# Second attention: high and low parts of the later heads spread over units, the other half's key rows copied on chip

## What is computed

```python
def diff_attend(q, k, v, lam):
    s = jnp.einsum('bqhmd,bkhmd->bhmqk', q, k, preferred_element_type=jnp.float32)
    a = jax.nn.softmax(s * (1.0 / math.sqrt(ATTN_HEAD_DIM)), axis=-1)
    a = a[:, :, 0] - lam * a[:, :, 1]
    return jnp.einsum('bhqk,bkhe->bqhe', a.astype(v.dtype), v)
```

## Time and profile before

| | us |
|---|---|
| median of 3 runs (2997.75 to 3001.31) | 2998.06 |
| profiled execution | 2997.38 |
| its span | 2996.1 |
| busy in the span: PE / DVE / ACT / POOL | 2786.9 / 1625.8 / 1218.2 / 289.7 |
| mean granted clock of PE | 0.973 |

### The profile page before, as it was taken

One profiled execution on the slowest core, in us unless ns is written; L12 is line 12 of the kernel. 1 busy time (PEld: TensorE's weight loads), 2 busy tenths in 40 slices (PEclk: granted clock), 3 DMA queues, 4 the chain that ended last, 5 costly groups with the idle time before them and its releaser, 6 DMA issues.

```text
span 2996.1 us, 36001 instructions
## 1 busy us (share of the span) xinstructions
PE 2786.9 (93%) x14288; PEld 2331.1 (78%) x14288; DVE 1625.8 (54%) x1933; ACT 1218.2 (41%) x1794; POOL 289.7 (10%) x397
## 2 busy tenths in 40 slices
PE   6999999999999999999999999978889399999994
PEld 5788888788888888888888888867778288888883
DVE  3277776432343323233334532367764688888985
ACT  3244443511232212122123412157762177777773
POOL 1011110000000000000002000023331300010002
PEclk9999999999999999999999999989999599999997
DMA  5100001111313222222232411000012589999994
GB/s 170 32 22 22 10 23 43 36 49 50 106 51 91 76 65 85 70 79 78 71 102 73 150 38 50 22 1 1 36 58 85 203 305 397 397 397 391 397 395 171
DMA packets 228103, 366.83 MB, mean 122 GB/s; under 512 B 11117, under 2 KB 158337, under 8 KB 227937
## 3 DMA queue, kind: packets, MB, share of 16 engines
q1 hardware_dynamic: 214688, 322.08, 30.4%
q0 software_dynamic: 13248, 42.45, 4.6%
HBM read 339.21 MB, written 25.28 MB: 122 GB/s over the span
## 4 chain that ended last, share of the span: by engine, by line
PE 73%; issue 16%; DVE 6%; ACT 2%; POOL 2%; DMA 1%; SPq 0%; ACTq 0%; DVEq 0%; POOLq 0%
PE ps L469 71%; DVE misc L2295 2%; POOL misc L947 1%; PE ps L548 1%; PE ps L2732 0%; PE ps L2753 0%; DVE r L2678 0%; ACT r L444 0%; DVE f L2619 0%; DVE f L2950 0%; DVE f L2617 0%; DVE f L2620 0%; DMA f<-in_x_dram 0%; ACT f L2218 0%; POOL f L2356 0%
## 5 line engine op out<-in xcount | busy, mean ns | idle before, releaser
L469 PE MATMUL ps<-r,r 128*128 128x512 f32 (+2 forms) x10824 | 2378.8, 377 | 27.3 <-DVE r L453 6.1
L469 PEld LDWEIGHTS ps<-r,r 128*128 128x128 f32 x10824 | 1928.4, 189 | 386.6 <-DVE r L453 12.5
L444 ACT ACTIVATE r<-f 128x1024 fp32r<-128x1024 f32 (+2 forms) x410 | 573.6, 1417 | 486.6 <-PE ps L469 484.3
L453 DVE TENSOR_TENSOR r<-f,r 128x1024 fp32r<-128x1024 f32 (+3 forms) x222 | 249.9, 1143 | 534.3 <-ACT r L444 534.1
L2678 DVE TENSOR_TENSOR r<-f,r 128x2048 fp32r<-128x2048 f32 x188 | 429.0, 2290 | 66.6 <-ACT r L444 65.3
L469 PE MATMUL ps<-f,f 128*128 128x128 f32 (+5 forms) x1538 | 245.6, 306 | 4.9 <-ACT f L2548 3.7
L469 PEld LDWEIGHTS ps<-f,f 128*128 128x128 f32 (+1 forms) x1538 | 204.2, 200 | 22.4 <-issue 15.7
L731 DVE SCALAR_TENSOR_TENSOR f<-f,misc,f 128x1023 f32<-128x1023 f32 (+29 forms) x120 | 146.3, 1261 | 0.0
L1583 ACT ACTIVATE r<-f 128x512 fp32r<-128x512 f32 x44 | 27.8, 632 | 210.1 <-DVE f L1605 210.1
L2218 ACT ACTIVATE f<-ps,misc 128x1280 f32<-128x1280 f32 x64 | 85.2, 1331 | 63.4 <-DVE misc L2295 63.4
L1015 ACT ACTIVATE f<-ps,misc 128x128 f32<-128x128 f32 (+7 forms) x64 | 47.5, 742 | 151.8 <-DVE misc L1004 151.8
(11 more groups left out here) (269 smaller groups left out, 1797.1 us busy)
## 6 DMA issues: line engine op xcount, KB each, us to landing
f<-in_w_gate_dram SPq DMA_DIRECT2D x64, 1024.0 KB, 8.3
f<-in_w_up_dram SPq DMA_DIRECT2D x64, 1024.0 KB, 10.4
f<-in_w_down_dram SPq DMA_DIRECT2D x64, 1024.0 KB, 8.2
f<-in_w_in_dram SPq DMA_DIRECT2D x56, 512.0 KB, 3.9
f<-in_w_ada_dram SPq DMA_DIRECT2D x48, 512.0 KB, 3.5
f<-in_w_ffn_in_dram SPq DMA_DIRECT2D x44, 512.0 KB, 4.7
f<-in_w_ffn_out_dram SPq DMA_DIRECT2D x18, 512.0 KB, 3.8
f<-in_w_out_dram SPq DMA_DIRECT2D x16, 512.0 KB, 3.5
```

The lines of the kernel that those rows point to most:

```text
L444: self.act.activation(st.hi[st.slot[i]][:, 0:n], st.raw[i % len(st.raw)][:, 0:n], ACT.Copy).then_inc(self.sem(st.name + "_hi"), 1)
L453: self.dve.tensor_tensor(st.lo[s][:, 0:n], st.raw[i % len(st.raw)][:, 0:n], st.hi[s][:, 0:n].bitcast(F32), ALU.subtract).then_inc(self.sem ...
L469: return self.pe.matmul(o, left, right, start=start, stop=stop, skip_group_check=True)
```

## The change

The high parts of the other rows are no longer made by ACT, and POOL's subtractions are gone. DMAs copy the own rows of K, L and C to the other rows: for head 0 on POOL's queue, for heads 1 to 3 on SP's, ahead of the loads of the output weights, which now wait for the high and low parts alone. PE waits for 96 counts (six DMAs) of `dma_k0` to `dma_k3` at a head's first scores. `act_stack` and `dve_stack` take a list of parts; the tables `HIGH_AT` and `LOW_AT` tell at which unit, counted from the start of the head before, each is made. For head 1 the high parts stand in units 2 to 5 and the low ones in 4 to 6; for heads 2 and 3 the high parts in units 1 to 5 and the low ones in 2 to 6 of the head before. For head 0 only the dealing of the work changes. Semaphores that share a number are regrouped.

```diff
@@ -1951,53 +1951,78 @@
 
 
 
-    def act_stack(self, h, mp):
-
-        act, sem = self.act, self.sem
+
+
+    HIGHS = [["Q0", "K0", "C0", "Q1", "K1", "C1"], ["K1", "C1", "Q0", "Q1", "K0", "C0"]] + 2 * [
+        ["Q0", "Q1", "K0", "C0", "C1", "K1"]]
+    LOWS = [["Q0", "K0", "C0", "Q1", "K1", "C1"], ["Q0", "Q1", "K1", "K0", "C0", "C1"]] + 2 * [
+        ["Q0", "Q1", "K0", "C0", "C1", "K1"]]
+
+    HIGH_AT = {2: "K1 C1", 3: "Q0", 4: "Q1", 5: "K0 C0"}, {1: "Q0", 2: "Q1", 3: "K0", 4: "C0 C1", 5: "K1"}
+    LOW_AT = {4: "Q0", 5: "Q1 K1", 6: "K0 C0 C1"}, {2: "Q0", 3: "Q1", 4: "K0", 5: "C0 C1", 6: "K1"}
+
+    def high_count(self, h, part):
+        return 6 * h + self.HIGHS[h].index(part) + 1
+
+    def low_count(self, h, part):
+        return 6 * h + self.LOWS[h].index(part) + 1
+
+    def stacked(self, h, part):
+
+        x, mp = part[0], int(part[1])
         own, other = ((slice(0, 64), slice(64, 128)), (slice(64, 128), slice(0, 64)))[mp]
         sk = self.stacks[h % 2]
-        act.activation(sk["Q"][mp][own, :], self.Q2[own, h, :], ACT.Copy).then_inc(sem("sk_hi"), 1)
-        for k, c in ((self.K2[own, h, :], slice(0, 1024)), (self.K2c[own, h, :], slice(1024, 1280))):
-            act.activation(sk["K"][mp][own, c], k, ACT.Copy).then_inc(sem("sk_hi"), 1)
-            act.activation(sk["K"][mp][other, c], k, ACT.Copy).then_inc(sem("sk_hi"), 1)
-
-    def low_keys(self, h, mp):
-
-        own = (slice(0, 64), slice(64, 128))[mp]
-        sk = self.stacks[h % 2]
-        return ((self.K2[own, h, :], sk["K"][mp][own, 0:1024], sk["L"][mp]),
-                (self.K2c[own, h, :], sk["K"][mp][own, 1024:1280], sk["C"][mp]))
-
-    def dve_low_queries(self, h, mp):
-
-        own, other = ((slice(0, 64), slice(64, 128)), (slice(64, 128), slice(0, 64)))[mp]
-        sk, n = self.stacks[h % 2], 5 * (2 * h + mp)
-        self.dve.wait_ge(*self.sem("sk_hi", n + 1))
-        self.dve.tensor_tensor(sk["Q"][mp][other, :], self.Q2[own, h, :], sk["Q"][mp][own, :].bitcast(F32),
-                               ALU.subtract).then_inc(self.sem("sk_lo"), 1)
-
-    def dve_low_keys(self, h, mp):
-
-        own = (slice(0, 64), slice(64, 128))[mp]
-        if h % 2 and mp:
-            self.dve.wait_ge(*self.sem("sk_lo", 3 * (2 * h + mp) + 1))
-        for j, (k, high, low) in enumerate(self.low_keys(h, mp)):
-            self.dve.wait_ge(*self.sem("sk_hi", 5 * (2 * h + mp) + 2 + 2 * j))
-            self.dve.tensor_tensor(low[own, :], k, high.bitcast(F32), ALU.subtract).then_inc(self.sem("sk_lo"), 1)
-
-    def pool_low_keys(self, h, mp):
-
-        other = (slice(64, 128), slice(0, 64))[mp]
-        if h % 2 and mp:
-            self.pool.wait_ge(*self.sem("sk_lo", 3 * (2 * h + mp) + 1))
-        for j, (k, high, low) in enumerate(self.low_keys(h, mp)):
-            self.pool.wait_ge(*self.sem("sk_hi", 5 * (2 * h + mp) + 2 + 2 * j))
-            self.pool.tensor_tensor(low[other, :], k, high.bitcast(F32), ALU.subtract).then_inc(self.sem("sk_lp"), 1)
-            self.pool.wait_ge(*self.sem("sk_lp", 2 * (2 * h + mp) + j + 1))
-
-    def dve_stack(self, h, mp):
-        self.dve_low_queries(h, mp)
-        self.dve_low_keys(h, mp)
+        if x == "Q":
+            return self.Q2[own, h, :], sk["Q"][mp][own, :], sk["Q"][mp][other, :], other
+        if x == "K":
+            return self.K2[own, h, :], sk["K"][mp][own, 0:1024], sk["L"][mp][own, :], other
+        return self.K2c[own, h, :], sk["K"][mp][own, 1024:1280], sk["C"][mp][own, :], other
+
+    def act_stack(self, h, parts):
+
+        for part in parts:
+            src, high, _, _ = self.stacked(h, part)
+            self.act.activation(high, src, ACT.Copy).then_inc(self.sem("sk_hi"), 1)
+
+    def dve_stack(self, h, parts):
+
+
+        for part in parts:
+            src, high, low, _ = self.stacked(h, part)
+            self.dve.wait_ge(*self.sem("sk_hi", self.high_count(h, part)))
+            if h == 1 and part == "K1":
+                self.dve.wait_ge(*self.sem("sk_lo", self.low_count(h, "Q1")))
+            self.dve.tensor_tensor(low, src, high.bitcast(F32), ALU.subtract).then_inc(self.sem("sk_lo"), 1)
+
+    def copy_high_keys(self, queue, h, mp):
+
+        other = self.stacked(h, f"K{mp}")[3]
+        own = slice(64 - other.start, 128 - other.start)
+        k = self.stacks[h % 2]["K"][mp]
+        queue.wait_ge(*self.sem("sk_hi", max(self.high_count(h, f"K{mp}"), self.high_count(h, f"C{mp}"))))
+        queue.dma_start(k[other, :].bitcast(F32), k[own, :].bitcast(F32)).then_inc(self.sem(f"dma_k{h}"), 16)
+
+    def copy_low_keys(self, queue, h, part):
+        other = self.stacked(h, part)[3]
+        own = slice(64 - other.start, 128 - other.start)
+        k = self.stacks[h % 2]["L" if part[0] == "K" else "C"][int(part[1])]
+        queue.wait_ge(*self.sem("sk_lo", self.low_count(h, part)))
+        queue.dma_start(k[other, :].bitcast(F32), k[own, :].bitcast(F32)).then_inc(self.sem(f"dma_k{h}"), 16)
+
+    def sp_stacks(self):
+
+        sp = self.sp
+        self.copy_high_keys(sp, 1, 1)
+        self.copy_low_keys(sp, 1, "K1")
+        self.copy_high_keys(sp, 1, 0)
+        for part in ("K0", "C0", "C1"):
+            self.copy_low_keys(sp, 1, part)
+        for h in (2, 3):
+            self.copy_high_keys(sp, h, 0)
+            for part in ("K0", "C0", "C1"):
+                self.copy_low_keys(sp, h, part)
+            self.copy_high_keys(sp, h, 1)
+            self.copy_low_keys(sp, h, "K1")
 
 
 
@@ -2022,8 +2047,7 @@
         act, sem = self.act, self.sem
         act.wait_ge(*sem("rp", 16))
         act.wait_ge(*sem("kc", 4))
-        self.act_stack(0, 0)
-        self.act_stack(0, 1)
+        self.act_stack(0, self.HIGHS[0])
         for ct in range(4):
             for n in range(3):
                 self.high(self.ws, self.i_cv + 3 * ct + n + 3)
@@ -2035,17 +2059,15 @@
 
     def dve_conv2(self):
         dve, sem, ps, u = self.dve, self.sem, self.ps, self.u2
-        self.dve_stack(0, 0)
-        self.dve_low_queries(0, 1)
+        self.dve_stack(0, ("Q0", "K0", "C0", "Q1"))
         for ct in range(4):
             o = self.CV[ct]
             self.low(self.ws, self.i_cv + 3 * ct + 4)
             if ct == 3:
 
                 dve.wait_ge(*sem("w_lo", len(self.ws.items)))
-                self.dve_low_keys(0, 1)
+                self.dve_stack(0, ("K1", "C1"))
                 dve.wait_ge(*sem("sk_lo", 6))
-                dve.wait_ge(*sem("sk_lp", 4))
             for hf in range(2):
                 dve.wait_ge(*sem("cv2_mm", 6 * ct + 2 + hf + 1))
                 dve.wait_ge(*sem("c2_u", 2 * ct + hf + 1))
@@ -2077,12 +2099,16 @@
             pool.dma_start(self.lams[:, i * 64:(i + 1) * 64], a[name].to_broadcast([P, 64])).then_inc(sem("lam"), 16)
 
     def pool_conv2(self):
-        self.pool_low_keys(0, 0)
+        pool = self.pool
+        self.copy_high_keys(pool, 0, 0)
+        self.copy_low_keys(pool, 0, "K0")
+        self.copy_low_keys(pool, 0, "C0")
+        self.copy_high_keys(pool, 0, 1)
         self.pool.wait_ge(*self.sem("mod_row", 4))
         self.pool.dma_start(self.rows_dram.rearrange("r (c p) -> (r c) p", p=P),
                             self.row_parts[0][64:96, :]).then_inc(self.sem("dma_kept"), 16)
-        self.pool.wait_ge(*self.sem("w_lo", len(self.ws.items)))
-        self.pool_low_keys(0, 1)
+        self.copy_low_keys(pool, 0, "K1")
+        self.copy_low_keys(pool, 0, "C1")
 
     def dve_lambda(self):
         dve, sem, lam, c, t = self.dve, self.sem, self.lams, self.lamc, self.lt
@@ -2137,9 +2163,9 @@
             if u:
                 pe.wait_ge(*sem(f"a2_exp{mp}", u))
             if i == 0:
-                pe.wait_ge(*sem("sk_hi", 5 * (2 * h + 2)))
-                pe.wait_ge(*sem("sk_lo", 3 * (2 * h + 2)))
-                pe.wait_ge(*sem("sk_lp", 2 * (2 * h + 2)))
+                pe.wait_ge(*sem("sk_hi", 6 * (h + 1)))
+                pe.wait_ge(*sem("sk_lo", 6 * (h + 1)))
+                pe.wait_ge(*sem(f"dma_k{h}", 96))
             q = sk["Q"][mp][:, i * P:(i + 1) * P]
             for c in range(3):
                 cs = slice(c * 512, min(c * 512 + 512, 1280))
@@ -2274,13 +2300,14 @@
                     act.wait_ge(*sem("cv2_mm", 24))
                 ct = (u + 3) % 4
                 act.activation(self.MX[0][:, 4 + ct, :], self.CV[ct], ACT.Copy).then_inc(sem("mc_hi"), 1)
-            for h, at in ((1, 4), (2, NT + 1), (3, 2 * NT + 1)):
-                if u == at:
-                    act.wait_ge(*sem("mc_lo", 4))
-                    act.wait_ge(*sem("a2_qk1", u + 1 if h == 1 else NT * (h - 1)))
-                    self.act_stack(h, 0)
-                if u == at + 1:
-                    self.act_stack(h, 1)
+            for h in range(1, 4):
+                parts = self.HIGH_AT[h > 1].get(u - NT * (h - 1), "").split()
+                if parts and h > 1:
+
+                    act.wait_ge(*sem("a2_qk1", NT * (h - 1)))
+                elif parts and u > 2:
```

(25 more changed lines are left out.)

## The result

The changed kernel takes 2972.51 us (median of 4 runs, 2970.34 to 2973.99) against 2999.68 (4 runs) for the kernel before: 27.2 us less, ratio 0.9900, 95% interval 0.9887 to 0.9912. Forecast were 33.7 less, 2964.4, with a range of 2958 to 2979. The sign and the mechanism were right, and so was the place but for unit 3, which the change made longer; 6.5 us of the gain are missing.

What follows compares the result with a forecast made beforehand. PE's matmuls were taken as 71% of the chain of waits, leaving only PE's waits in the stack stretches to win; gains of 11.3, 11.3 and 11.1 us off 2998.06 gave 2964.4 us, range 2958 to 2979.

Steps and rivals of the forecast that it cites:

- Where the loss sits: Second attention, units 4 to 24: stretches holding stacks of heads 1 to 3 exceed plain 6.34 us units by 43.1 us.
- High parts, 3.1 us a head: Heads 2 and 3: ACT's remaining high parts lie in both unit loops; 3.1 us a head stay, bounds 2.5 to 5.0.
- Low parts, nothing: DVE's low parts, a unit after their high parts, cost nothing, covered by its 1.28 us wait for PE's first scores.
- rival B: Stack units: each high part with its low part still costs 2.2 us, fifteen cost 33, gain 10: 2988 us; 6%.
- Copies hidden: On-chip copies before each head's first scores: last lands in 3.2 us against 4.8 of room, so nothing is waited for.
- Rivals C and D: Head starts: C, last copy lands late, 2985 us, 9%; D, a copy runs on one DMA engine, 3040 us, 3%.
- Heads 2 and 3: Units 9 to 16 and 17 to 24: 64.95 us becomes about 53.8; gains 11.3 and 11.1 us.
- Head 1: Units 4 to 8: 34.6 us for 46.24, less 0.3 lost earlier; gain 11.3, between 9.5 and 12.5.
- K1 C1 in unit 2 ... +0.2 to 0.3: Units 2 and 3: head 1's high parts delay ACT's next copies, partly covered by 1.32 us idle; +0.2 to 0.3 us.
- Rival A: Fifteen stack units: short PE idles drop its clock to 1.2 GHz, 0.9 us a unit, 14 us: 2978 us; 12%.
- Sum: Whole kernel: gains of 11.3, 11.3 and 11.1 us for heads 1, 2 and 3 make 33.7, arriving whole: 2964.4 us.

Runs made afterwards that it cites:

- copies alone: Changed kernel with on-chip copies kept, but high and low parts bunched again into two units a head, lows with their highs: 2988.84 us, ratio 0.9958.
- spreading alone: Changed kernel with parts still spread over units, but heads 1 to 3 without copies: ACT makes high keys twice, POOL subtracts again; 2994.75 us, ratio 0.9977.

## Why the prediction was right, and where it was off

**Where the loss sits** held. The gain lies in the stretches of heads 1 to 3, and the 43.1 us there were the ceiling; outside them only unit 3 moved, 1.1 us the wrong way.

**Both halves at once.** The forecast priced high and low parts together, not the halves of the change. The runs show: copies alone 12.8, spreading alone 8.0, together 28.3. Each half alone leaves a loss that the other takes away: with the copies alone DVE still waits 2.87 us for ACT's first high part, with the spreading alone POOL's subtractions hold up DVE and PE stands for ACT's double copies. How the 7.5 us between 20.8 and 28.3 divide over these was not measured.

**High parts, 3.1 us a head**, held. From the first reduction of unit 9 to that of unit 15 six units take 41.33 us (2034.40 to 2075.73), 3.3 more than six plain ones of 6.34, for 3.1. The reason held too, since moving them out of the loop took 4.2 us off head 2, 3.0 without its unit 16.

**Low parts, nothing**, held for heads 2 and 3: no unit is more than 0.02 us shorter when they are all but left out, and 21.1 us for two heads are lost when the cover of one unit is taken away. That is 2.1 us for each of ten units, near the 2.2 of rival B, which didn't come here because the low part stands a unit behind.

**Copies hidden** held: 2.9 us for the last where I took 3.2, against 5.2 of room. Rivals C and D are out.

**Heads 2 and 3: 55.35 and 55.34 for 53.8.** The term that was too small is "3.1 us a head stay": it left out what follows the last stack unit. Unit 16 is 7.80 us, because POOL's product and DVE's mix start together; 1.2 us a head with the product away. The row was there to be found: the kernel before had units of 7.9 us behind its own stack units, and PE waited for POOL in them (unit 20 above). I took them for catching up and never asked what PE waited for. By the Trainium skill, SBUF — State Buffer, "Who interferes with whom", DVE and GpSimd share a port pair that is an exclusive lock; the 1.92 for 0.61 us of POOL and the 3.26 for 1.55 of DVE agree. I used that for the subtractions of the kernel before and not for the small product that stays.

**Head 1: 36.16 for 34.6, and unit 3 10.26 for 9.12.** Unit 3 lies ahead of head 1's stretch, but the forecast counted it there. Of the 1.56 us too much in the stretch 0.7 are unit 8, where POOL's product is held up as in unit 16, and 1.0 is unit 5, forecast 8.1 and measured 9.09 at a clock of 0.81; the other three units give 0.1 back. For unit 3 the term "K1 C1 in unit 2 ... +0.2 to 0.3" was too small: ACT's idle 1.32 us was counted, PE's standing was not. With 1.19 us already there and 1.47 more PE stood 2.72 us. With a clock near the one before (0.82) that costs 0.4 us, as three kernels show that make head 1's parts as the changed kernel does: PE stands 2.71 or 2.72 us in them, and unit 3 is 9.49. The other 0.8 is a longer spell of low clock, 0.70 instead of 0.82 over the unit, and the low clock itself was there before the change (0.85). So 1.5 us in units 3 and 5 (10.2 and 9.1, or 9.5 and 8.3) come and go with the execution. In the seven profiles that make head 1's parts in this way they go with the clock in unit 0, long in the four where it is 1.00, short in the three where it is 0.79 to 0.82; why is not shown. High parts out of PE's way give 9.12 in unit 3 and 8.35 in unit 5.

**Rival A** had the mechanism, and in the wrong place: heads 2 and 3 keep 1.00 in both profiles of the changed kernel, with waits of 0.76 to 1.20 us in their stack units, and the clock falls around head 1. But it was argued away with too little. The 1.19 us at full clock of the earlier trace rows are one profile's: in unit 29, which neither the change nor any edit but those of POOL's product touches, the clock is 1.00 in nine of the fourteen profiles and 0.84 or 0.85 in five. There the scores are slow although the waits just ahead are 0.79, 0.73 and 0.25 us; the unit is 11.19 us long in place of 10.56. In the changed kernel's second profile:

```profile
2176.82 0.44 PE L2184 MATMUL ps<-misc,f 128*128 128x128 f32 x2 [0.25 <-ACT f L2257]
2177.01 2.19 PE L469 MATMUL ps<-r,r 128*128 128x512 f32 x6
```

And 1.19 us in unit 3 of the kernel before was followed by scores of 2.48. So the reading in the prediction that the trace disagrees with a clock that swings on short idles is wrong as a general one: the length of the single wait does not tell whether the clock falls.

**Sum.** 11.3, 11.3 and 11.1 were 8.9 (unit 3 included), 9.8 and 9.6: 28.3 in the attention, 5.4 less than forecast. Of these 3.1 are the held-up product in units 8, 16 and 24, and 1.8 are units 3 and 5. Between the 28.3 and the 27.2 us of the medians lie 0.5 us behind the attention and 0.6 that a few runs can't tell from chance.

## What to carry to other kernels

Work that is to be hidden on a busy engine has to stand where that engine waits, and the row to look for is its own idle time in brackets; the same 5 us of high parts cost 3.3 us a head behind the values copy and 0.4 ahead of the exponential. When a producer and a consumer on two in-order engines are in the same loop, try a unit of delay between them first: taking it away cost 21.1 us here, while leaving out the consumer's work gained nothing. And when an estimate says that an engine's idle time takes the added work, ask at once how long the matmul engine then stands, and whether its clock was low there already, for the clock is the second price and it differs between executions of one kernel.

## What the hardware showed

A copy of 64 partitions to the other 64, 256 KB, lands 2.9 us after its issue on SP's queue, 320 KB in 3.2 us; on POOL's queue 3.0 and 4.1. With several on the way PE saw nothing of them.

DVE and POOL hold each other up in both directions. A POOL product of 128 x 128, 0.61 us alone, takes 1.92 when it starts 0.02 us behind a DVE mix of 1.55; the same mix takes 3.26 when a POOL subtraction of 2.37 us started 0.46 us before it. What DVE does matters: behind one of its subtractions of 128 x 1024 the product takes 1.64 to 1.66 us, and beside its reduction, whose input is in PSUM (`ps`), 0.61. ACT's product takes 0.40 to 0.41 us in all 32 units, beside the mix or not.

The granted clock (1.00 is 2.4 GHz) stayed at 1.00 in the ten stack units of heads 2 and 3 with PE waits of 0.76 to 1.20 us. Scores ran at the time of 1.2 GHz (2.48 for 1.40 us) after waits of 2.72 us, but also after one of 1.19 us in the kernel before. The same instructions in unit 29 ran at 1.00 in nine profiles and at 0.84 or 0.85 in five.
